# A 31-tap depthwise convolution: from two swapped halves on TensorE to four shifted copies with 16 taps a chunk

## The reference

```python
def conformer_conv(x, w_pw1, b_pw1, dw_w, dw_b, ln_g, ln_b, w_pw2, b_pw2):
    a = x @ w_pw1 + b_pw1
    u = a[..., :D_MODEL] * jax.nn.sigmoid(a[..., D_MODEL:])
    u = lax.conv_general_dilated(u, dw_w[:, None, :], window_strides=(1,),
        padding=[(CONV_WIDTH - 1, 0)], dimension_numbers=("NWC", "WIO", "NWC"),
        feature_group_count=D_MODEL) + dw_b
    u = jax.nn.silu(layer_norm(u, ln_g, ln_b))
    return u @ w_pw2 + b_pw2
```

## Time and profile before

| | |
|---|---|
| median of 3 runs | 2512.59 us (2512.54 to 2512.70) |
| span of the profiled execution, first to last instruction | 2511.1 us |
| own time of the profiled execution | not listed apart from its span |
| granted TensorE clock, mean | 0.999 |
| the stage of the convolution's taps | about 34 to 153 us |

### The profile page before, as it was taken

The page is one execution under the profiler, slowest core; times in us unless marked ns, Lnnn a source line. Parts: engine busy times, 40 slices in busy tenths (PEclk is TensorE's granted clock), DMA queues, the critical chain, the costliest instruction groups (busy, mean ns, idle before and its releaser), DMA issues.

```text
span 2511.1 us, 32123 instructions
## 1 busy us (share of the span) xinstructions
PE 2471.5 (98%) x11922; PEld 1977.5 (79%) x11922; DVE 1366.6 (54%) x2154; ACT 997.5 (40%) x1402; POOL 1104.1 (44%) x555
## 2 busy tenths in 40 slices
PE   8999999999999999999999999999999999999998
PEld 5658888888778788888876878888889758888887
DVE  6975644644566556365337665651554465652553
ACT  5563322234655532223334253532434344532333
POOL 6854444444323344444443423544445313544443
PEclk9999999999999999999999999999999999999999
DMA  5215546534221355464343312323323122324322
GB/s 150 71 62 162 190 148 189 180 94 120 84 79 56 91 186 183 143 200 152 88 137 93 93 51 76 84 80 113 101 75 102 60 72 68 84 77 116 96 77 71
DMA packets 398714, 273.53 MB, mean 109 GB/s; under 512 B 10195, under 2 KB 381907, under 8 KB 398588
## 3 DMA queue, kind: packets, MB, share of 16 engines
q1 hardware_dynamic: 384764, 221.52, 30.8%
q10 hardware_dynamic: 13824, 50.34, 5.4%
HBM read 269.70 MB, written 2.12 MB: 108 GB/s over the span
## 4 chain that ended last, share of the span: by engine, by line
PE 89%; DVE 6%; ACT 3%; issue 1%; POOL 1%; DMA 0%; DVEq 0%; SPq 0%; ACTq 0%
PE ps L716 27%; PE ps L718 26%; PE ps L717 26%; DVE ps L2240 2%; PE ps L1499 1%; PE ps L1103 1%; PE ps L1077 1%; PE ps L1216 1%; PE ps L1062 1%; PE ps L1065 1%; PE ps L1339 1%; PE ps L1191 1%; DVE u_lo L1677 1%; PE ps L1441 0%; ACT weight_hi L2640 0%
## 5 line engine op out<-in xcount | busy, mean ns | idle before, releaser
L2498 POOL TENSOR_TENSOR weight_lo<-weight_raw,weight_hi 128x1024 fp32r<-128x1024 f32 (+3 forms) x417 | 944.2, 2285 | 1323.0 <-ACT weight_hi L2640 1200.4
L718 PE MATMUL ps<-u_hi,weight_lo 128*128 128x512 f32 (+1 forms) x2456 | 929.0, 378 | 0.0
L716 PE MATMUL ps<-u_hi,weight_hi 128*128 128x512 f32 (+1 forms) x2248 | 879.1, 391 | 9.1 <-DVE u_lo L1573 2.2
L717 PE MATMUL ps<-u_lo,weight_hi 128*128 128x512 f32 (+1 forms) x2248 | 868.1, 386 | 0.0
L2640 ACT ACTIVATE weight_hi<-weight_raw 128x2048 fp32r<-128x2048 f32 (+2 forms) x213 | 363.2, 1705 | 574.2 <-PE ps L718 542.3
L718 PEld LDWEIGHTS ps<-u_hi,weight_lo 128*128 128x128 f32 x2456 | 461.8, 188 | 87.0
L716 PEld LDWEIGHTS ps<-u_hi,weight_hi 128*128 128x128 f32 x2248 | 422.3, 188 | 117.8 <-issue 16.5
L717 PEld LDWEIGHTS ps<-u_lo,weight_hi 128*128 128x128 f32 x2248 | 422.4, 188 | 86.3 <-issue 2.9
L718 PE MATMUL ps<-act_hi,weight_lo 128*128 128x512 f32 (+1 forms) x748 | 281.5, 376 | 0.0
L716 PE MATMUL ps<-act_hi,weight_hi 128*128 128x512 f32 (+1 forms) x704 | 269.5, 383 | 0.0
L717 PE MATMUL ps<-act_lo,weight_hi 128*128 128x512 f32 (+1 forms) x704 | 269.2, 382 | 0.0
(11 more groups left out here) (341 smaller groups left out, 2731.5 us busy)
## 6 DMA issues: line engine op xcount, KB each, us to landing
weight_raw<-in_ffn_w_up SPq DMA_DIRECT2D x132, 512.0 KB, 5.2
arena<-in_ada_w ACTq DMA_DIRECT2D x96, 512.0 KB, 5.7
weight_raw<-in_ffn_w_down SPq DMA_DIRECT2D x64, 704.0 KB, 4.5
weight_raw<-in_ffn_w_gate SPq DMA_DIRECT2D x44, 512.0 KB, 4.1
weight_raw<-in_ev_w_in SPq DMA_DIRECT2D x10, 1024.0 KB, 5.5
weight_raw<-in_conv_w_pw SPq DMA_DIRECT2D x16, 512.0 KB, 5.8
weight_raw<-in_ple_w_gate SPq DMA_DIRECT2D x16, 512.0 KB, 3.7
weight_raw<-in_attn_w_qkv SPq DMA_DIRECT2D x16, 512.0 KB, 5.2
```

The costliest lines, as they stand in the source:

```text
L716: pe.matmul(bank, w[0], x[0], start=start, stop=False)
L717: pe.matmul(bank, w[0], x[1], start=False, stop=False)
L718: return pe.matmul(bank, w[1], x[0], start=False, stop=stop)
L2498: low_part = pool.tensor_tensor(w_lo[r][:, cols], raw[r][:, cols], w_hi(k0 + j)[:, cols].bitcast(F32), ALU.subtract)
```

## The change

TensorE does 16 taps of every chunk. After the gate of a chunk, SyncE copies it inside SBUF in 16 transfers: channels come in four quarters of 32, and for quarter j and shift k the channels of quarter j, moved by k tokens, go to partitions 32k to 32k + 31 of `shifted`. One product of 128 rows and 32 columns then sums four taps of 32 channels, and the four quarters go to four column strips. A chunk has four groups of four taps: 16 products. There are two `shifted` buffers, and a chunk's copies wait until the taps of the chunk two before are done. TensorE waits for all 16 copies.

The taps of chunk c - 1 now come after both tiles of slot c, not between them. The swap bank, ScalarE's swap and its semaphore go, and pw1's tiles use four banks, not three. VectorE has taps 16 to 23 (16 to 25 in the last chunk), adds TensorE's bank to its own sum in `conv_finish`, after the fourth tap of the next chunk, and sums squares at the end of a chunk. GpSimd builds 16 blocks of 32 columns a chunk from the `fold` constant. On SyncE's queue, pw1 slots 4 to 7 and pw2's four slots are loaded each behind a chunk's copies, and `bias_rows` comes ahead of the first copies. The parameter array keeps its width (8 x 15 columns of taps and 128 of tap rows for 8 x 31).

```diff
-PE_TAPS = (10, 10, 8, 10, 8, 10, 10, 16)
+SHIFTS = 4
+TAP_GROUPS = (4, 4, 4, 4, 4, 4, 4, 4)
+PE_TAPS = tuple(SHIFTS * g for g in TAP_GROUPS)
+OWN_FROM = min(PE_TAPS)
...
-            for j in range(DC):
+            for j in range(RING):
                 load("pw1", pair(a["conv_w_pw1"], a["conv_w_pw1"], 0, D), only=j)
...
             sp.dma_start(bias_rows, act[0:HEADS, 20 * S:20 * S + 640]).then_inc(bias_stored, 16)
-            load("pw2", plain(a["conv_w_pw2"]))
+
+            def shift_copies(c):
+
+                width = S + SHIFTS * (TAP_GROUPS[c] - 1)
+                sp.wait_ge(conv_in_ready, c + 1)
+                if c >= 2:
+                    sp.wait_ge(pe_taps_done, c - 1)
+                for j in range(SHIFTS):
+                    for k in range(SHIFTS):
+                        sp.dma_start(shifted_part(c, j, 0, width)[quarter(k)],
+                                     conv_in[c % 3][quarter(j), k:k + width]).then_inc(shifts_landed[c % 2], 16)
+
+            for c in range(DC):
+                shift_copies(c)
+                if c < DC - RING:
+                    load("pw1", pair(a["conv_w_pw1"], a["conv_w_pw1"], 0, D), only=c + RING)
+                else:
+                    load("pw2", plain(a["conv_w_pw2"]), only=c - RING)
...
-                pe.wait_ge(conv_in_ready, c + 1)
-                pe.wait_ge(diag_early_built if c < 5 else diag_late_built, c + 1 if c < 5 else c - 4)
+                pe.wait_ge(shifts_landed[c % 2], 16 * SHIFTS * SHIFTS * (c // 2 + 1))
+                pe.wait_ge(diagonals_built, c + 1)
                 if 2 <= c < DC - 1:
                     pe.wait_ge(pe_taps_used, c - 1)
-                if c:
-                    pe.wait_ge(swap_copied, 2 * c)
-                x, last = conv_in[c % 3], PE_TAPS[c] - 2
-                for t in range(0, PE_TAPS[c], 2):
-                    for k, bank, rows_of in ((t, tap_bank(c), (lower, upper)), (t + 1, swap_bank, (upper, lower))):
-                        for r, to in zip((lower, upper), rows_of):
-                            mm = pe.matmul(bank[to], tap_diag(c, k)[r], x[r, k:k + S], start=t == 0, stop=t == last)
+                for g in range(TAP_GROUPS[c]):
+                    for j in range(SHIFTS):
+                        mm = pe.matmul(tap_bank(c)[quarter(j)], tap_weights(c, g, j), shifted_part(c, j, SHIFTS * g, S),
+                                       start=g == 0, stop=g == TAP_GROUPS[c] - 1)
                 mm.then_inc(pe_taps_done, 1)
...
-                        if i == 0:
-                            pe_taps(c - 1)
+                    pe_taps(c - 1)
...
+                for t in taps:
+                    x = cin[:, t:t + S]
+                    if t == taps[0]:
+                        link(dve.tensor_scalar(own, x, tap(t), None, ALU.mult))
+                    else:
+                        link(dve.scalar_tensor_tensor(y if t == taps[-1] else own, x, tap(t), own, ALU.mult, ALU.add))
+                    if t == taps[3] and c:
                         conv_finish(c - 1)
...
             def conv_finish(c):
 
+                dve.wait_ge(pe_taps_done, c + 1)
+                link(dve.tensor_tensor(tap_bank(c), tap_bank(c), chunk(conv_out, c), ALU.add))
                 dve.wait_ge(side_added, side_adds[c + 1])
...
+            def build_diagonals(c):
+                n_, at = TAP_GROUPS[c] * SHIFTS, PARAM_AT["conv_tap_rows"] + SHIFTS * group_base[c]
+                pool.tensor_tensor(diagonals[:, group_base[c] * P:group_base[c + 1] * P].rearrange("p (t n) -> p t n", t=n_),
+                                   const("fold").unsqueeze(1).to_broadcast([P, n_, QUARTER]),
+                                   par[:, at:at + n_].unsqueeze(2).to_broadcast([P, n_, QUARTER]), ALU.mult).then_inc(diagonals_built, 1)
...
-            def swap(c):
-
-                sc.wait_ge(pe_taps_done, c + 1)
-                if c >= 2:
-                    sc.wait_ge(pe_taps_used, c - 1)
-                sc.activation(swapped[c % 2][lower], swap_bank[upper], ACT.Copy).then_inc(swap_copied, 1)
-                sc.activation(swapped[c % 2][upper], swap_bank[lower], ACT.Copy).then_inc(swap_copied, 1)
```

More of the change, by code:

```diff
@@ L48 @@
 BANKS = 4
-CONV_BANKS = 3
-OWN_TAPS = 9
 HALF = P // 2
+QUARTER = P // SHIFTS
 SLOT = 2048
@@ L59 @@
 PARAM_WIDTHS = [
-    ("conv_norm_g", 8), ("conv_b_pw1", 16), ("conv_dw_w", 8 * CONV), ("conv_dw_b", 8),
+    ("conv_norm_g", 8), ("conv_b_pw1", 16), ("conv_dw_w", 8 * (CONV - OWN_FROM)), ("conv_tap_rows", SHIFTS * sum(TAP_GROUPS)), ("conv_dw_b", 8),
     ("conv_ln_g", 8), ("conv_ln_b", 8), ("conv_b_pw2", 8), ("attn_norm_g", 8),
@@ L353, in build @@
         PADW = CONV - 1 + S
+        SHIFTED = S + SHIFTS * (max(TAP_GROUPS) - 1)
         conv_in = [act[:, i * PADW:(i + 1) * PADW] for i in range(3)]
@@ L470, in build @@
         side_used = sem("side_used")
-        diag_early_built, diag_late_built = sem("diag_early_built"), sem("diag_late_built")
+        diagonals_built = sem("diagonals_built")
+        shifts_landed = [sem(f"shifts_landed{s}") for s in range(2)]
         pe_taps_done = sem("pe_taps_done")
         pe_taps_used = sem("pe_taps_used")
-        swap_copied = sem("swap_copied")
         xn_ready = sem("xn_ready")
@@ L2218, in conv_taps @@
                 taps = range(PE_TAPS[c], CONV - SIDE_TAPS[c])
[L2219 to L2227, removed]
-                        conv_finish(c - 1)
[L2229 to L2243, removed]
+                tap = lambda t: pcol("conv_dw_w", c * (CONV - OWN_FROM) + t - OWN_FROM)
+                own, y = ps[:, 6], chunk(conv_out, c)
+                for t in taps:
[5 more added lines that the diff above has]
+                    if t == taps[3] and c:
+                        conv_finish(c - 1)
+                if c:
+                    square_sum(c - 1)
             def conv_finish(c):
+                dve.wait_ge(pe_taps_done, c + 1)
+                link(dve.tensor_tensor(tap_bank(c), tap_bank(c), chunk(conv_out, c), ALU.add))
                 dve.wait_ge(side_added, side_adds[c + 1])
@@ L3105, in _ @@
                 for i in range(SIDE_TAPS[c]):
-                    tap = pcol("conv_dw_w", c * CONV + CONV - SIDE_TAPS[c] + i)
+                    tap = pcol("conv_dw_w", (c + 1) * (CONV - OWN_FROM) - SIDE_TAPS[c] + i)
                     x = conv_in[c % 3][:, CONV - SIDE_TAPS[c] + i:CONV - SIDE_TAPS[c] + i + S]
@@ L3118, in _ @@
                     sc.activation(side_prod[m % 3], x, ACT.Copy, scale=tap).then_inc(side_ready, 1)
-                    if i == 3 and c:
+                    if i == 4 and c:
                         conv_square(c - 1)
[L3121 to L3124, removed]
+                if c == DC - 1:
+                    ln_table_ahead()
             split_after("pw1", Step(DC - 1))
@@ L3358, in taps_last, with tap_rows @@
         return np.reshape(w, (w.shape[0], -1, P)).transpose(2, 1, 0).reshape(P, -1)
+    def tap_rows(w):
+        turned = np.reshape(w, (CONV, DC, SHIFTS, QUARTER))
+        rows = [turned[SHIFTS * g:SHIFTS * (g + 1), c].transpose(0, 2, 1).reshape(P, SHIFTS) for c in range(DC) for g in range(TAP_GROUPS[c])]
+        return np.concatenate(rows, axis=1)
     def twice(v):
```

44 lines of the change are left out of this document (17 added, 27 removed).

## The result

The changed kernel takes 2517.09 us (median of 20 runs) and the kernel before, run beside it, 2512.84: a ratio of 1.0016, 95% interval 1.0009 to 1.0022. That is 4.25 us slower; the forecast was 0.6 us faster. It lies in the range of 2507 to 2521 and within the 0.2% taken as no change, but its sign is the other one. The profiled execution's span went from 2511.1 to 2516.4 us.

What follows compares the result with a forecast made beforehand. TensorE, busy for 98% of the span, was taken as the bound. A hand-over to the last sums 2.6 us earlier and 2.0 us for a clock drop gave -0.6 us: 2512.0 us timed, range 2507 to 2521.

Steps and rivals of the forecast that it cites:

- What bounds the kernel, and the shift of one instant: TensorE, busy 98%, bounds the kernel; everything behind the hand-over to the last sums at 148.47 is unchanged, so its shift counts.
- TensorE's block of 3.6 us: A chunk's 16 products in four 128x32 column strips take 3.6 us; TensorE gets 7.8 us less work.
- rivals 3 and 4: TensorE's strips run two abreast, 2534 us, chance 0.07; or partly abreast, block of 4.3 us, 2516.9 us, chance 0.05.
- VectorE, ScalarE, GpSimd off the path: TensorE is full beside them, so their saved work becomes idle time, VectorE's some 5 us a chunk; late GpSimd weights cost nothing.
- Covered in the middle, not at the ends: Copies need 11.0 us after a slot, covered by the 14.70 us period; TensorE waits 0.2 us first and 5.5 us last.
- The copies, X = 0.1 + 15 x 0.49 + 1.8 = 9.3: Copy time from a chunk's gate to last landing on SyncE's queue: 9.3 us, copies 0.49 apart, landing 1.8; bounds 6.8 and 13.1.
- 2X - 21.2: Shift in us from copy time X, from 9.1 up to 13, before the clock; first and last stall both follow X.
- The forecast's own sign of being wrong: In the new profile, copies more than 0.65 us apart or landing later than 4 us would show the forecast wrong.
- The clock: TensorE's idle 5.5 us before chunk 7's taps likely drops its granted clock: 2.0 us added, bounds 0 and 3.6.
- Rival 1: Slow copies on SyncE's queue, 0.64 us apart, landing 3.4, X = 13.1: +6.9 us with the clock, 2519.5 us; chance 0.17.
- Sum: Hand-over to the last sums 2.6 us earlier, plus 2.0 for the clock: -0.6 us, 2510.5 in the profile, 2512.0 timed.

Runs made afterwards that it cites:

- e6: Changed kernel with the taps of chunk c-1 put back between the two tiles of slot c: 2589.07 us, one execution.
- e5: Changed kernel without copies for chunk 7, whose taps on TensorE read chunk 6's copies (not the reference's sums): 2508.72 us, one execution.
- e3: Changed kernel with each of the 16 copies moving 256 tokens, not 524, which taps read twice (not the reference's sums): 2516.16 us, one execution.
- e4: Changed kernel with four 128-partition copies a chunk for sixteen of 32, same bytes, rows in another order (not the reference's taps): 2505.70 us, one execution.
- e2: Changed kernel with ScalarE's queue issuing 8 of the 16 copies of chunks 0 and 7: 2510.17 us, 0.9988 of the kernel before.
- e1: Changed kernel with throwaway products on TensorE ahead of its two waits for copies: 2514.58 us, 1.0006 of the kernel before.
- e9: Changed kernel with four copies a chunk, each reading 32 channels at four shifts, nothing left out: 2510.98 us, 0.999 of the kernel before.
- e7: Changed kernel with the token sums of chunks 2 to 6 also moved ahead of chunk 7's taps: 2513.23 us, 1.0001 of the kernel before.

## Why the prediction was wrong

- **What bounds the kernel, and the shift of one instant:** right. All of the change is at the hand-over to the last sums.
- **TensorE's block of 3.6 us:** right, 3.57 at full clock, so rivals 3 and 4 are out: 32 instructions in four 128x32 strips take what 32 in quadrants did (3.59). The Trainium skill's 2.38 of 3 ("TensorE: Matmul & The Clock Gate", Part 3), an estimated 4.3 us here, does not show.
- **VectorE, ScalarE, GpSimd off the path:** right. The time freed became waits for the sigmoid (37.8 us in eight chunks, 4.7 each, some 5 said), and TensorE never waited for GpSimd's splits.
- **Covered in the middle, not at the ends:** right, the period 14.67 (14.70 said); e6 takes the cover away and e5 the last wait.
- **The copies, X = 0.1 + 15 x 0.49 + 1.8 = 9.3:** this step failed; the term that was mis-sized is the 0.49 us between two copies. The forecast weighed two rows and took the stores' 0.49 apart because they too start in SBUF; the copies come 0.635 apart, as the position loads do (0.64), and the last lands 2.1 after its issue: 0.2 + 15 x 0.635 + 2.1 = 11.8, of which the pitch is 2.2 of the 2.5 missing. By the forecast's own formula that is 2X - 21.2 = +2.4 in place of -2.6: paid twice, as a first wait of 2.57 (0.2 said) that also makes every later slot late, and a last of 7.76 (5.5 said). e3 shows that issue and not bytes sets it, e4 that the count of copies does, e2 that it is the queue. The forecast's own sign of being wrong, copies more than 0.65 apart, was set too wide to catch 0.635.
- **The clock:** the price was near (1.7 a time, 2.0 said), the count was not. It fell behind the first wait also, which was to be only 0.2 us long: +3.4 in place of +2.0. Rival 1 too, with 3.9 us of first wait, counted one drop. e1 gives these 3.4 back in the profile, 2.5 in the medians.
- **Sum:** +2.4 + 3.4 = +5.8 by the formula, +5.2 measured in the profile (six periods 0.03 shorter each, the last X 11.7 and the first gate 0.1 earlier make up most of the difference), +4.25 in the timed runs. (What lies around the span was taken as 1.5 us; the profiled execution of the change has 2518.19 - 2516.4 = 1.8.) The cause is rival 1's, with its pitch and not its landing of 3.4, which is why it came out less slow than its 2519.5. That the time still lies in the stated range is no credit to the sum: the range was drawn wide enough to take in rival 1.

What stays open is how the timed executions differ among themselves. The change's profile has 5.3 and its medians 4.25, but the profiled execution took 2518.19 us, 1.1 above the median of its 20. e2's profiled one took 2508.54, the shortest of its 11, which is why its span fell by 9.7 and its median by 6.9. The eleven lie in two groups: four at 2508.54 to 2508.95 us with a mean granted clock of 0.999, seven at 2510.12 to 2512.22 with 0.998, 1.75 us apart by their medians. That is near the price of one clock drop, so in most executions of e2 the clock may well have fallen once; no trace of one of these exists, so it is not shown. It would fit that the change has 0.997 in 18 of 20 and e1 0.999 in 10 of 11.

## What to carry to other kernels

Where one queue's issue sets the pace, as here, cost a series of DMAs as their count times the pitch plus one landing, and where two rows give different pitches, carry both to the end: here 0.145 us on the pitch, over 15 steps and two bare waits, was 4.4 us. A transfer in a pipeline is free in the middle and bare at both ends, so price the first and the last chunk by themselves, each with the clock drop that a wait can bring. Then look for independent work behind the last wait that can stand in it (3.9 us here for one moved block), and for a form with fewer transfers.

## What was not expected of the hardware

- A plain copy inside SBUF costs its queue 0.59 to 0.61 us (medians), whether it moves 32 partitions of 256 floats, of 524, or 128 partitions of 524 (e3, the change, e4). From ScalarE it is 0.61, and eight of them hold that engine's arithmetic for 5.11 us (e2).
- The source matters. 268 KB written to 128 partitions land 2.6 us after issue from 128 partitions and 5.0 us from 32 partitions read four times with overlap (e4, e9), and the issue of one grows from 0.61 to as much as 1.8 us.
- How long TensorE idled did not by itself tell whether the clock dropped: it fell around waits of 2.57 (the change) and 3.46 us (e7), and stayed at 1.00 through 2.37 (e3) and 3.12 us (e2), each in the one execution that was profiled. When it had fallen, the block behind took 5.0 to 6.6 us in place of 3.57.
